# Four gated feed-forward blocks computed as 2 x 2 x 2 block products with seven quarter products, and their down projection in three runs of k tiles

## The reference, cut to what matters

```python
c_act = silu(c)
mod = (c_act @ mod_w[i] + mod_b[i])            # 9 vectors of 1024 per layer: shifts, scales, gates
h = modulate(rms_norm(x, norm_g[i, 0]), sh0, sc0)
x = x + 0.5 * g0 * swiglu(h, ffn_w_gu[i, 0], ffn_w_down[i, 0])
# swiglu: g, u = split(h @ w_gu); return (silu(g) * u) @ w_down     1024 -> 2 x 2816 -> 1024
# then the mixer: pooling (layer 0) or differential attention (layer 1), then a second swiglu
```

## Time and profile before

| | |
|---|---|
| median of three runs | 2855.75 us (2853.83 to 2864.46) |
| profiled execution, span of its instructions | 2868.0 us |
| mean granted TensorE clock | 0.986 |
| matmuls | 16211 |
| four gated blocks, windows in the span | 1047 to 1414, 1455.5 to 1822, 1825 to 2191.5, 2483.5 to 2850 |

### The profile page before, as it was taken

How to read it: one execution, slowest core, us unless ns; L and a number is a source line. 1 busy time by engine, 2 the same in 40 slices (tenths; PEclk the granted TensorE clock), 3 DMA queues, 4 the chain that set the end, 5 groups by cost and what they waited for, 6 DMA issues and landing times.

```text
span 2868.0 us, 40754 instructions
## 1 busy us (share of the span) xinstructions
PE 2783.2 (97%) x16211; PEld 2249.2 (78%) x16211; DVE 1428.6 (50%) x2059; ACT 979.6 (34%) x1530; POOL 241.9 (8%) x318
## 2 busy tenths in 40 slices
PE   8999888999999999999989999999999999999998
PEld 7855777887887878888878888788887866788887
DVE  4588643666776455555443332433324876433322
ACT  3355443333332232222342222322223265422222
POOL 1000110112000111001110000100002300100000
PEclk8899999999999999999999999999999999999999
DMA  6331001673332655566323333233333310233332
GB/s 234 115 99 59 3 3 32 218 229 118 102 93 87 204 152 195 186 199 197 100 68 95 95 95 98 88 95 95 92 101 97 108 37 23 77 100 95 93 94 70
DMA packets 89844, 311.07 MB, mean 108 GB/s; under 512 B 11632, under 2 KB 12400, under 8 KB 89584
## 3 DMA queue, kind: packets, MB, share of 16 engines
q1 hardware_dynamic: 66928, 232.62, 26.0%
q0 software_dynamic: 22784, 76.56, 8.7%
HBM read 305.99 MB, written 2.10 MB: 107 GB/s over the span
## 4 chain that ended last, share of the span: by engine, by line
PE 91%; DVE 4%; ACT 3%; issue 1%; POOL 1%; DMA 1%; SPq 0%; DVEq 0%; ACTq 0%; POOLq 0%
PE psum L1924 24%; PE psum L1926 24%; PE psum L1925 24%; PE psum L2101 1%; PE psum L2103 1%; PE psum L2102 1%; PE psum L2612 1%; PE psum L2601 1%; PE psum L1999 1%; PE psum L1995 1%; PE psum L1996 1%; PE psum L2303 1%; PE psum L2076 1%; PE psum L2392 1%; PE psum L2273 1%
## 5 line engine op out<-in xcount | busy, mean ns | idle before, releaser
L1144 DVE TENSOR_TENSOR w_lo<-stage,w_hi 128x1024 fp32r<-128x1024 f32 (+2 forms) x441 | 518.3, 1175 | 827.4 <-ACT w_hi L655 827.2
L655 ACT ACTIVATE w_hi<-stage 128x1024 fp32r<-128x1024 f32 (+2 forms) x441 | 449.7, 1020 | 1206.1 <-PE psum L1926 1171.7
L1924 PE MATMUL psum<-h_hi,w_hi 128*128 128x512 f32 (+1 forms) x2024 | 792.7, 392 | 3.3 <-DVE w_lo L1144 2.3
L1925 PE MATMUL psum<-h_lo,w_hi 128*128 128x512 f32 (+1 forms) x2024 | 790.9, 391 | 0.0
L1926 PE MATMUL psum<-h_hi,w_lo 128*128 128x512 f32 (+1 forms) x2024 | 790.5, 391 | 0.0
L1924 PEld LDWEIGHTS psum<-h_hi,w_hi 128*128 128x128 f32 (+1 forms) x2024 | 381.1, 188 | 86.7 <-DVE w_lo L1144 4.4
L1926 PEld LDWEIGHTS psum<-h_hi,w_lo 128*128 128x128 f32 (+1 forms) x2024 | 381.0, 188 | 80.2
L1925 PEld LDWEIGHTS psum<-h_lo,w_hi 128*128 128x128 f32 (+1 forms) x2024 | 381.1, 188 | 79.6
L1924 PE MATMUL psum<-hid_hi,w_hi 128*128 128x512 f32 x880 | 344.0, 391 | 6.5 <-DVE hid L1234 6.5
L1926 PE MATMUL psum<-hid_hi,w_lo 128*128 128x512 f32 x880 | 343.4, 390 | 0.0
L1925 PE MATMUL psum<-hid_lo,w_hi 128*128 128x512 f32 x880 | 343.2, 390 | 0.0
(11 more groups left out here) (440 smaller groups left out, 3023.0 us busy)
## 6 DMA issues: line engine op xcount, KB each, us to landing
stage<-in_up SPq DMA_DIRECT2D x220, 512.0 KB, 3.6
mod_w<-in_mod_w POOLq DMA_DIRECT2D x144, 512.0 KB, 4.3
stage<-in_down SPq DMA_DIRECT2D x80, 448.0 KB, 3.3
stage<-in_down SPq DMA_DIRECT2D x40, 512.0 KB, 3.5
stage<-in_w_in SPq DMA_DIRECT2D x24, 512.0 KB, 3.6
stage<-in_w_qkv SPq DMA_DIRECT2D x24, 512.0 KB, 3.6
stage<-in_w_merge SPq DMA_DIRECT2D x16, 512.0 KB, 4.5
turned_n<-in_cmp_w SPq DMA_DIRECT2D x1, 4096.0 KB, 13.1
```

What stands on the lines that cost most here:

```text
L655: act.activation(w_hi[:, c % 2, 0:kt * cols], stage[:, c % NSTAGE, 0:kt * cols], ACT.Copy).then_inc(hi_done, 1)
L1144: dve.tensor_tensor(w_lo[:, c % 2, 0:kt * cols], stage[:, c % NSTAGE, 0:kt * cols], w_hi[:, c % 2, 0:kt * cols].bitcast(F32), ALU.subtract ...
L1924: pe.matmul(dst, wh[:, n], a_hi[:, k], start=start and n == 0, stop=False)
L1925: pe.matmul(dst, wh[:, n], a_lo[:, k], start=False, stop=False)
```

## The change

In f = 1 to 4 the pair of output tiles (2 x 128 rows), the k tiles taken in pairs, and the tokens in two halves of 256 form a 2 x 2 x 2 block product. Winograd's form of Strassen's scheme makes it of seven quarter products. A block becomes 34 items in one order (`ITEMS`): 9 ups, 4 downs over k tiles 0 to 7, 8 ups, 4 downs over 8 to 15, 5 ups, 4 downs over 16 to 21. Each item is two weight units and, for downs, two output tiles. The first two ups (PLAIN) are computed as before; all others go through `seven_block`: seven products with 256 moving columns, each over 4 (or 3) k pairs and with three matmuls per pair.

The four quarter matrices of the weights of an item are used in four groups: Y (one quarter), X (two), S (two) and T (two). Y and X are the loaded weights themselves; S and T are made by POOL in the stage slots by four additions or subtractions (`sums_a` behind the low part of Y, `sums_b` behind the low part of X). ACT rounds each group and DVE takes its low part, in two rings: X and S in `w_hi`, T and Y in the new `w2_hi`. PE does T4 with Y, then B11 and B21 with X, T1 and T3 with S, T2 and B22 with T.

The moving side has sums as well: for the ups DVE makes them once per block from h (h now kept in float32 in `h32`); for the downs POOL makes four of 256 columns for each pair of hidden tiles (`pair_sums`), ACT rounds and DVE takes the low parts (`round_pair`, `low_pair`). The products land in four PSUM banks per item, two sets by turns; ACT copies one half (`take_first`) and DVE combines the rest by four additions (`collect`) before SiLU, the product for hid, or the two adds to xT. The partial sums of a down projection are added to xT after each of its three runs.

The mod tiles move: 33 to up0, 36 to down0 (two behind a weight unit in 15 of its 24, one in six), 11 to the downs of f = 1. DVE's up0 loop is written out instead of looped.

```diff
+CHUNKS = [(0, 8), (8, 8), (16, 6)]
...
+ITEMS = ([("up", p) for p in range(9)] + [("down", 0, q) for q in range(4)] + [("up", p) for p in range(9, 17)]
+         + [("down", 1, q) for q in range(4)] + [("up", p) for p in range(17, 22)] + [("down", 2, q) for q in range(4)])
+PLAIN = 2
...
+PLAIN_BANKS = [(3, 4), (6, 7)]
+SEVEN_BANKS = [(0, 1, 2, 5), (3, 6, 7, 4)]
...
-        order += [("up1", up, 44), ("down1", down, 8), ("pool", [(2, 2 * P)] * 4, 8),
-                  ("up2", up, 44), ("down2", down, 8), ("up3", up, 44), ("down3", down, 8),
-                  ("qkv", [(KD, P)] * 24, 24), ("attn_out", [(KD, P)] * 8, 8),
-                  ("up4", up, 44), ("down4", down, 8)]
+        ffn = [(KD if item[0] == "up" else CHUNKS[item[1]][1], P) for item in ITEMS for _ in range(2)]
+        order += [("ffn1", ffn, 52), ("pool", [(2, 2 * P)] * 4, 8), ("ffn2", ffn, 52), ("ffn3", ffn, 52),
+                  ("qkv", [(KD, P)] * 24, 24), ("attn_out", [(KD, P)] * 8, 8), ("ffn4", ffn, 52)]
...
-        MOD_AT = {"mix_in": 0, "merge": 25, "mix_out": 57, "down0": 64, "up1": 85, "down1": 129}
+        UP_RUNS = [(0, 1), (1, 9), (10, 1)]
+
+        MOD_AT = {"mix_in": 0, "merge": 25, "mix_out": 57, "up0": 64, "down0": 97, "ffn1": 133}
+
+        def mods_down(idx):
+
+            first = MOD_AT["down0"] + idx + min(idx, 15)
+            return range(first, first + (2 if idx < 15 else 1)) if idx < 21 else ()
...
+            def sums_a(f, idx):
+
+                g, c, nk = seven(f, idx), unit_pair(f, idx), pairs_of(ITEMS[idx])
+                (a11, _), (a21, a22) = quarters(c, nk), quarters(c + 1, nk)
+                pool.wait_ge(s_lo, 3 * g + 1)
+                pool.tensor_tensor(a22, a21, a22, ALU.add).then_inc(s_sum, 1)
+                own(4 * g + 1)
+                pool.wait_ge(loaded[c % NSTAGE], 16 * (c // NSTAGE + 1))
+                pool.tensor_tensor(a21, a21, a11, ALU.subtract).then_inc(s_sum, 1)
+
+            def sums_b(f, idx):
+
+                g, c, nk = seven(f, idx), unit_pair(f, idx), pairs_of(ITEMS[idx])
+                (a11, a12), (_, s1) = quarters(c, nk), quarters(c + 1, nk)
+                pool.wait_ge(s_lo, 3 * g + 2)
+                own(4 * g + 2)
+                pool.tensor_tensor(a11, s1, a11, ALU.subtract).then_inc(s_sum, 1)
+                own(4 * g + 3)
+                pool.tensor_tensor(a12, a12, a11, ALU.subtract).then_inc(s_sum, 1)
+
+            def pair_sums(f, p):
+
+                j, at = p // 2, 4 * (KPAIRS * (f - 1) + p // 2)
+                b1, b2 = R[0][:, S:2 * S], R[1][:, S:2 * S]
+                T = RD[:, j % 2].rearrange("p (a n) -> p a n", a=4)
+                pool.wait_ge(hid_done, PAIR[f] + p + 1)
+                pool.tensor_tensor(T[:, 0], b1[:, HALF:S], b1[:, 0:HALF], ALU.subtract).then_inc(t_made, 1)
+                pool.tensor_tensor(T[:, 1], b1[:, HALF:S], b2[:, HALF:S], ALU.subtract).then_inc(t_made, 1)
+                pool.wait_ge(t_made, at + 1)
+                pool.tensor_tensor(T[:, 2], b2[:, HALF:S], T[:, 0], ALU.subtract).then_inc(t_made, 1)
+                pool.wait_ge(t_made, at + 3)
+                pool.tensor_tensor(T[:, 3], b2[:, 0:HALF], T[:, 2], ALU.subtract).then_inc(t_made, 1)
+
...
+                    if is_seven(idx + 1) and not tail(idx):
+                        sums_a(f, idx + 1)
+                    if odd_tile(idx - 1):
+                        pair_sums(f, ITEMS[idx - 1][1])
+                    if tail(idx):
+                        sums_a(f, idx + 1)
+                    if is_seven(idx + 1):
+                        sums_b(f, idx + 1)
...
+                i = act.activation(weights(which, c, nk)[0], src, ACT.Copy)
+                if which == "T":
+                    i.then_inc(hi_done, 2)
+                else:
+                    i.then_inc(s_hi, 1)
...
+                C = R[par] if item[0] == "up" else RD[:, par]
+                act.activation(C[:, HALF:S], psum[:, SEVEN_BANKS[par][3], 0:HALF], ACT.Copy).then_inc(p1_out, 1)
...
+            def low_weights(which, f, idx):
+
+                g, c, nk = seven(f, idx), unit_pair(f, idx), pairs_of(ITEMS[idx])
+                src = {"Y": quarters(c + 1, nk)[1], "X": stage[:, c % NSTAGE, 0:2 * nk * P],
+                       "S": stage[:, (c + 1) % NSTAGE, 0:2 * nk * P], "T": stage[:, c % NSTAGE, 0:2 * nk * P]}[which]
+                hi, lo_ = weights(which, c, nk)
+                if which == "T":
+                    dve.wait_ge(hi_done, c + 2)
+                    dve.tensor_tensor(lo_, src, hi.bitcast(F32), ALU.subtract).then_inc(lo_done, 2)
+                else:
+                    dve.wait_ge(s_hi, 3 * g + "YXS".index(which) + 1)
+                    dve.tensor_tensor(lo_, src, hi.bitcast(F32), ALU.subtract).then_inc(s_lo, 1)
+
+            def collect(f, idx):
+
+                g, c, par = seven(f, idx), unit_pair(f, idx), idx % 2
+                b0, b1, b2, _ = SEVEN_BANKS[par]
+                C = (R[par] if ITEMS[idx][0] == "up" else RD[:, par]).rearrange("p (a n) -> p a n", a=4)
+
+                def halves(b):
+                    return psum[:, b, :].rearrange("p (a n) -> p a n", a=2)
+
+                one = C[:, 1].unsqueeze(1).to_broadcast([P, 2, HALF])
+                dve.wait_ge(p1_out, g + 1)
+                dve.wait_ge(s_six, g + 1)
+                dve.tensor_tensor(C[:, 0:4:3], one, halves(b0), ALU.add).then_inc(s_ev, 1)
+                dve.wait_ge(s_ev, 4 * g + 1)
+                dve.tensor_tensor(C[:, 1:3], C[:, 3].unsqueeze(1).to_broadcast([P, 2, HALF]), halves(b1),
+                                  ALU.add).then_inc(s_ev, 1)
+                dve.wait_ge(s_ev, 4 * g + 2)
+                dve.tensor_tensor(C[:, 3], C[:, 2], halves(b1)[:, 0], ALU.add).then_inc(s_ev, 1)
+                dve.wait_ge(s_ev, 4 * g + 3)
+                dve.wait_ge(unit_done, c + 2)
+                dve.tensor_tensor(C[:, 1:3], C[:, 1:3], halves(b2), ALU.add).then_inc(s_ev, 1)
+
...
+                for idx in range(1, len(ITEMS) + 1):
+                    if idx == PLAIN:
+                        low_t(f, 3)
+                    if is_seven(idx - 1):
+                        collect(f, idx - 1)
+                    if is_seven(idx + 1) and not tail(idx):
+                        low_weights("Y", f, idx + 1)
+                    if is_seven(idx):
+                        low_weights("T", f, idx)
+                    if kind_of(idx - 1) == "up":
+                        p = ITEMS[idx - 1][1]
+                        dve.wait_ge(silu_done, PAIR[f] + p + 1)
+                        other = R[p % 2][:, S:2 * S]
+                        if idx - 1 < PLAIN:
+                            dve.wait_ge(unit_done, unit_pair(f, idx - 1) + 2)
+                            other = psum[:, PLAIN_BANKS[idx - 1][1], :]
+                        dve.tensor_tensor(R[p % 2][:, S:2 * S], R[p % 2][:, 0:S], other, ALU.mult).then_inc(hid_done, 1)
+                    elif kind_of(idx - 1) == "down":
+                        _, chunk, q = ITEMS[idx - 1]
+                        dve.wait_ge(s_ev, 4 * seven(f, idx - 1) + 4)
+                        for e in range(2):
+                            m = 2 * q + e
+                            dve.scalar_tensor_tensor(out=xT[:, m], in0=RD[:, (idx - 1) % 2, e * S:e * S + S], scalar=gate(m),
+                                                     in1=xT[:, m], op0=ALU.mult,
+                                                     op1=ALU.add).then_inc(x_ready if chunk == 2 else s_x, 1)
+                    if is_seven(idx + 1) and not tail(idx):
+                        low_weights("X", f, idx + 1)
+                    if odd_tile(idx - 1):
+                        low_pair(f, ITEMS[idx - 1][1], 0)
+                    if is_seven(idx + 1) and not tail(idx):
+                        low_weights("S", f, idx + 1)
+                    if odd_tile(idx - 1):
+                        low_pair(f, ITEMS[idx - 1][1], 1)
+                    if tail(idx):
+                        for which in "YXS":
+                            low_weights(which, f, idx + 1)
+                    if kind_of(idx - 1) == "down" and f == 1 and downs < 11:
+                        mod(MOD_AT["ffn1"] + downs)
+                        downs += 1
...
+                        mod(MOD_AT["up0"] + 3 * i + 2 * q)
...
-                        if s.name in MOD_AT and n < KD - 1:
-                            mod(MOD_AT[s.name] + 3 * n + j)
+                        for t in mods_down(3 * n + j):
+                            mod(t)
...
+            def seven_block(f, idx):
+
+                g, c, par, item = seven(f, idx), unit_pair(f, idx), idx % 2, ITEMS[idx]
+                nk = pairs_of(item)
+                b0, b1, b2, b3 = SEVEN_BANKS[par]
+                (xh, xl), (yh, yl), (sh, sl), (th, tl) = [
+                    [w.rearrange("p (n m) -> p n m", m=P) for w in weights(which, c, nk)] for which in "XYST"]
+
+                def from_h(name, j):
+                    if name in ("B21", "B22"):
```

(66 more changed lines are left out.)

367 lines of the change are left out of this document (273 added, 94 removed).

## The result

The changed kernel takes 3121.38 us (median of 4 runs, 3118.12 to 3121.63); the kernel before, on the same chip, 2854.79. The ratio is 1.0912 (95% interval 1.0879 to 1.0944). The direction was forecast; the size was not: 3007 was predicted, with 3070 as the upper end. The profiled execution has a span of 3119.6 us.

What follows compares the result with a forecast made beforehand. PE, 97% busy, was taken to bound the kernel before. Four blocks (+121) and moved mod tiles (+18, +2, +10) gave +151 on 2868.0 us, 3019, less 12 for the median: 3007; range 2820 to 3070, likeliest 2950 to 3065.

Steps and rivals of the forecast that it cites:

- the two engines shut each other out: DVE and POOL: while one streams two SBUF tensors the other stands still; a POOL sum holds DVE about 1.07 us.
- cycle of two ups: Steady seven-product ups in a block: an even and an odd item together 23.5 to 25.2 us, taken as 24.5.
- spacing of matmuls: PE: matmul starts lie 226.7 ns apart at 512 columns and 119.6 ns at 256, so halving columns leaves 53%.
- The floor of the forecast: Two up items: DVE's work plus POOL's held time, less at most all of `collect` hidden: 22.1 us against PE's 20.1.
- sum of +151: Whole kernel: +121 us for four blocks and +18, +2 and +10 for moved mod tiles, on the profiled 2868.0 us.
- `Head` and `Tail`: Block's start waits for a low unit, 3 us; its end has `collect` and two adds before the last squares, 2 us.
- The first down of the third run: Six-tile downs: the first waits for the last hidden pair, 8.2 us under 5.0 of matmul cover, 10.7 us in all.
- Mod tiles: Moved tiles: DVE waits for slot refills, +18 us in down0; +2 in up0; +10 in block 1's downs.
- Rival A: Blocks: DVE and POOL get by each other, so PE's count decides; 2805 us, or 2787 without down0's wait; chance 0.17.
- The clock (C): Odd up items: PE's pauses of 3 to 4 us cost the clock, up to 68 us more, 3075 us; chance 0.05.
- D: Whole kernel: PE stays the bound and small gains meet new waits, within 0.5%, 2842 to 2870 us; chance 0.06.
- B: Ups: the lock holds, but POOL's sums fall under `collect` and waits nearly always; 22.1 us a cycle, 2911 us; chance 0.15.

Runs made afterwards that it cites:

- one-operand kernel: Changed kernel with each POOL sum replaced by a multiplication by 1.0 reading one operand, sums left out, waits kept: 3080.07 us in one run.
- moved roundings: Changed kernel with T's three roundings put before hi of the run's second weight at a block's head: 3117.69 us, 1.0903.
- short memsets: Changed kernel with POOL's weight and pair sums replaced by rows of 64-column memsets (0.79 us a sum), sums left out, waits kept: 2872.81 us, 1.0054.
- two passes of memsets: Changed kernel with each weight sum replaced by eight 64-column memsets done twice (1.60 us), pair sums thrice, sums left out: 3031.72 us, 1.0607.

## Why the prediction was right in its direction and short in its size

The mechanism held: the two engines shut each other out, and the steady cycle of two ups had the length forecast. The step that failed is in the sum: the terms for the ends of a block, for the first downs behind a run of ups and for the mod tiles were too small, together by some 110 us. The parts follow.

**The spacing of matmuls held.** In the changed kernel the 256-column matmuls start 119 ns apart, as in the earlier trace rows; the timeline of PE:

```profile
1918.53 0.28 PE L2347 MATMUL psum<-HB,w_lo 128*128 128x256 f32 x1
1918.64 0.28 PE L2345 MATMUL psum<-HB,w_hi 128*128 128x256 f32 x1
1918.76 0.28 PE L2346 MATMUL psum<-HB,w_hi 128*128 128x256 f32 x1
```

**That the two engines shut each other out held**, and it decided: with memsets of about the sums' unheld length and nothing held 2897 us; with it 3121. DVE's timeline in the changed kernel, beside POOL's:

```profile
1600.83 1.22 DVE L1507 TENSOR_TENSOR w_lo<-stage,w_hi 128x1024 fp32r<-128x1024 f32 x1
1601.97 1.78 DVE L1589 TENSOR_TENSOR norm_t<-norm_t 128x512 f32<-128x512 f32 x1
1603.67 3.56 DVE L1510 TENSOR_TENSOR w_lo<-stage,w_hi 128x1024 fp32r<-128x1024 f32 x2
```

```profile
1601.00 2.20 POOL L663 TENSOR_TENSOR stage<-stage 128x512 f32<-128x512 f32 x1 [2.02 <-DVE w_lo L1510]
1603.28 1.61 POOL L666 TENSOR_TENSOR stage<-stage 128x512 f32<-128x512 f32 x1
```

The sum of L663 starts under the first `w_lo` and takes 2.20 us; hid (L1589), queued behind, then stands by for it and takes 1.78 us for its 0.69.

**The cycle of two ups was right in number (24.5 for 24.45), the downs too (10.1 for 10.2).** The floor of the forecast, 22.1 us, was 16.7 of DVE's own work and 5.4 in which it is held; measured are 16.6 (with memsets) and 5.2, 21.8 together. In the other 2.65 us of the cycle DVE is idle, mostly waiting for ACT (1.73 of it behind the pair sums). The forecast had such waits in its timetable, which passed through both engines in turn. That it hit the number within 0.05 us is in part luck: the items alternate at 9.4 and 15.05 us, where 10.55 (or 9.5) and 14.6 (or 13.5) were given, and 24.5 was a choice between 23.5 and 25.2.

What the first expectations read it as, DVE's work plus the time it is held, is only a part of it. A held POOL sum delays S and T: DVE's low part of Y releases the sums, these ACT's rounding, this DVE's low part, and that PE's matmuls. DVE's lengthening alone, two thirds of it, gives 20.5 us; POOL's alone gives 22.7 at 1.60 us a sum, both 22.9. The last 1.5 us up to 24.45 were not separated by memsets, for these kernels had less of both: POOL 18.2 us of sums for 19.6, DVE 20.3 us for 21.8. The one-operand kernel points to the sums' length: POOL busy for 19.9 us, DVE for 17.6, and two ups of 24.15.

**Terms that were mis-sized**, against the sum of +151 on the profiled execution. The span came out 100.6 us over the 3019.
- *The two ends of a block* (`Head` and `Tail`). Forecast 369.1 + 30.2 = 399.3 for a block, measured 421: 21.7 too few. 12.3 of it lie outside the 31 steps from the first `collect` to the last, where 3 and 2 us had been allowed. At the head PE waited 3.79 us for the low part of a plain weight, and the matmuls behind it ran 427 ns apart for 5 us, at the lower clock (granted clock 0.50 from 1574.5 to 1579.0 us), which costs 2.4 us more; 3 us had been allowed for both:

```profile
1569.99 0.39 PE L2266 MATMUL psum<-h_two,w_lo 128*128 128x512 f32 x1
1574.16 0.79 PE L2264 MATMUL psum<-h_two,w_hi 128*128 128x512 f32 x1 [3.79 <-DVE w_lo L1381]
1574.76 0.63 PE L2265 MATMUL psum<-h_two,w_hi 128*128 128x512 f32 x1
1575.18 0.63 PE L2266 MATMUL psum<-h_two,w_lo 128*128 128x512 f32 x1
```

Another 3.4 us are the first item's fill (15.6 us from its first matmul to its `collect`, counted as 12.25). The rest, some 6 us, is the tail: the last matmul of the block's products starts 12.7 us before the next stage, for 3.7 before the change, and of that PE waits 5.42 us for the sum of squares behind the last `collect` and its adds to xT:

```profile
1962.97 1.87 PE L2279 MATMUL psum<-cst,rexp 128*128 128x1 f32 x8 [5.42 <-POOL rexp L640]
```

The order at the head is not the reason, as the moved roundings showed. Nor is the hold the reason for the tail: from the last `collect` to the next stage it is 11.6 us here and 10.3 to 11.9 in all kernels with memsets. The first `collect` of block 2 comes 49.9 us into it here and 44.4 with short memsets, so a part of the head does depend on the sums.
- *The first down of the third run*: 17.0 us for 10.7. PE had done the 42 matmuls of its cover and then waited for the last pair's low part:

```profile
1919.59 0.28 PE L2347 MATMUL psum<-HB,w_lo 128*128 128x256 f32 x1
1924.75 0.58 PE L2345 MATMUL psum<-HB,w_hi 128*128 128x256 f32 x1 [4.88 <-DVE HB L1547]
```

It is 12 to 14 us with memsets of up to 0.99 us, 16.2 at 1.34 us, 18.4 at 1.60 and 20.4 at 2.42: the pair's chain has POOL in it four times over, and was priced too short even with sums that nothing holds.
- *The first downs of the other runs*: 12.2 us each for 10.1; with the downs behind them, at 9.9 to 10.4, 4.7 us a block.
- *Mod tiles.* down0 +28.6 for +18, up0 +8.5 for +2, block 1 +18 (438.9 less 421) for +10: 25 us too few in all. Two of the three lay over the upper end given for them (25 and 14). The mechanism for FFN0 was right: DVE waited 37.6 us for tiles that had not landed, and 36 us of FFN0 went when the added tiles were left out. The size was not; landing took 4.7 us in the median, near the 4.6 assumed, but up to 7.3, which may be why and isn't shown.

Together 65 (blocks 2 to 4), 30 (block 1 with its mod tiles) and 17 (FFN0); the mixer of this profile, 13 us shorter, hides some of it. Rival A's sum has the same terms: its cycle came with short memsets, and the time was 2873 us for 2805, 68 too few. So the larger part of what is missing is there without the hold. The ends of runs were given one value each, and terms of 2 to 12 us a block that all erred the same way had no place in the upper end.

**The clock (C)** did fall: 0.93 in a cycle of two ups, 1.00 before. With two passes of memsets it was 0.91 at 22.7 us and, with DVE's additions, 1.00 at 22.9. The windows of one cycle in each, columns as above; in the first of them matmul records are missing (126 for 168):

```profile
1616.43:1639.13 22.70, 16.81 (x126) 16.40 (x124) 16.55 (x23) 10.34 (x14) 16.82 (x177) 0.91 0.31 93
```

```profile
1600.00:1622.90 22.90, 21.66 (x184) 21.45 (x182) 20.32 (x38) 10.99 (x15) 16.83 (x178) 1.00 0.28 94
```

The kernel of two passes has both by itself: of its first three cycles of 22.7 us in block 2 the granted clock is 0.92, 1.00 and 0.91. So in the steady ups the clock sets nothing; at the head of a block it cost the 2.4 us named above. **A and D** are out, though A's cycle of 20.1 us is what came once POOL's sums were short. **B** (2911) wanted 22.1 us for two ups with the sums under `collect`; 22.2 came only when half of the weight sums and the pair sums had gone to DVE, and then the time was 3005.

## What to carry to other kernels

Before you move vector work to GpSimd beside a busy VectorE, price each pair of operations with two SBUF operands as taking turns, on both engines, and then lay the longer durations along the chain that runs through both: a helper that is busy for 70% of the block, as POOL was here, and has to be waited for twice per item can set the cycle. Halving the columns of a matmul saved 47% here and not half, so a scheme that trades eight products for seven has 7.6% to spend on everything it adds. When a forecast is a sum of many terms, give each head, tail and first item of a run its own line and its own upper end.

## What the runs showed of the hardware

- Who holds whom depends on the operand count of the POOL operation. POOL sums of two SBUF operands lengthened DVE's `w_lo` (1506 ns on average). Operations of a single operand hardly lengthened that of X and S (1231 ns) and lengthened others less (T's 1303; the hid product 1.1 us for 0.69, and 1.7 beside two operands), but were themselves lengthened from 1.49 us to 2.4. Memsets did neither (1225). The Trainium skill (GPSIMD Engine Reference, Key points) says that GpSimd contends with VectorE's instructions that have two SBUF inputs. The trace agrees as to VectorE's side: the additions with a PSUM operand kept 687 ns, and the hid product, which has two SBUF operands now, went to 1747.
- A one-operand multiplication on 512 columns took POOL 1.49 us, a two-operand subtraction 1.29.
- Memsets in a row start closer than they last: 64 columns are shown as 150 ns, and sixteen take 1.57 us, 98 ns each.
- A matmul of 256 columns at the lower clock starts 213 ns after its predecessor and not 239, twice 119.6; one of 512 columns 427 (in the rows at 1574 us) for 226.7 at the higher.

```profile
1604.08 0.41 PE L2345 MATMUL psum<-h_two,w_hi 128*128 128x256 f32 x1
1604.29 0.41 PE L2346 MATMUL psum<-h_two,w_hi 128*128 128x256 f32 x1
1604.50 0.41 PE L2347 MATMUL psum<-h_two,w_lo 128*128 128x256 f32 x1
```
